# Attention's values for the middle column blocks by DMA, and its first two projection units a stage earlier

## What is computed

```python
h = _rms(x, pre_g) * (1 + scale) + shift                     # for latent and context tokens
q, k, v, g = split(h @ w_in)                                 # 16 heads of 64
s_win = einsum(q, k[row_sel]) * scale + bias                 # window: 8 rows x 16 columns, masked by column
s_ctx = einsum(q, k_ctx) * scale
p = softmax(concat(s_win, s_ctx))
o = einsum(p_win, v[row_sel]) + einsum(p_ctx, v_ctx)
out = (o * silu(g)) @ w_out
```

## Time and profile before

| | us |
|---|---|
| median of 3 runs | 2271.32 (2268.11 to 2275.94) |
| the profiled execution | 2274.24 |
| its span, first to last instruction | 2272.4 |

### The profile page before, as it was taken

How to read it: one execution, slowest core, us unless ns; L and a number is a source line. 1 busy time by engine, 2 the same in 40 slices (tenths; PEclk the granted TensorE clock), 3 DMA queues, 4 the chain that set the end, 5 groups by cost and what they waited for, 6 DMA issues and landing times. The chain is left out here.

```text
span 2272.4 us, 35679 instructions
## 1 busy us (share of the span) xinstructions
PE 2086.1 (92%) x12490; PEld 1717.3 (76%) x12490; DVE 1396.0 (61%) x3285; ACT 1133.4 (50%) x2790; POOL 468.8 (21%) x452
## 2 busy tenths in 40 slices
PE   4699999999999999999976999699999999999797
PEld 2488888787878878787755888577877877877676
DVE  4475968879596887969584433414554554555652
ACT  4244747566573856657363332324544444444431
POOL 1012323233232323323220111310110110110300
PEclk9799999999999999999987999899999999999799
DMA  9512322222221212122127434221211211211433
GB/s 372 202 58 77 98 72 93 74 75 66 83 92 47 102 66 82 60 84 96 38 79 242 126 101 128 65 62 47 71 45 54 74 49 47 75 47 38 151 80 86
DMA packets 118685, 204.70 MB, mean 90 GB/s; under 512 B 29021, under 2 KB 79197, under 8 KB 116461
## 3 DMA queue, kind: packets, MB, share of 16 engines
q1 hardware_dynamic: 106988, 160.47, 22.4%
q10 hardware_dynamic: 11520, 41.95, 5.4%
HBM read 175.69 MB, written 28.65 MB: 90 GB/s over the span
## 5 line engine op out<-in xcount | busy, mean ns | idle before, releaser
L419 PE MATMUL sg_pP<-h_h_hi,h_whi 128*128 128x512 f32 (+1 forms) x1152 | 428.8, 372 | 0.0
L421 PE MATMUL sg_pP<-h_h_hi,h_wlo 128*128 128x512 f32 (+1 forms) x1152 | 410.1, 356 | 0.0
L420 PE MATMUL sg_pP<-h_h_lo,h_whi 128*128 128x512 f32 (+1 forms) x1152 | 409.0, 355 | 0.0
L419 PE MATMUL at_pP<-h_h_hi,at_whi 128*128 128x512 f32 (+1 forms) x640 | 254.4, 397 | 8.4 <-POOL at_wlo L2180 8.4
L421 PEld LDWEIGHTS sg_pP<-h_h_hi,h_wlo 128*128 128x128 f32 x1152 | 218.7, 190 | 31.5
L420 PEld LDWEIGHTS sg_pP<-h_h_lo,h_whi 128*128 128x128 f32 x1152 | 219.4, 190 | 29.6
L419 PEld LDWEIGHTS sg_pP<-h_h_hi,h_whi 128*128 128x128 f32 x1152 | 219.2, 190 | 29.2 <-issue 0.2
L421 PE MATMUL at_pP<-h_h_hi,at_wlo 128*128 128x512 f32 (+1 forms) x640 | 239.0, 374 | 0.0
L420 PE MATMUL at_pP<-h_h_lo,at_whi 128*128 128x512 f32 (+1 forms) x640 | 237.5, 371 | 0.0
L864 ACT ACTIVATE sg_S<-sg_rowb,sg_tab 128x128 f32<-128x128 f32 x640 | 195.9, 390 | 60.9 <-DVE sg_E L1126 56.1
L2180 POOL TENSOR_TENSOR at_wlo<-h_wr,at_whi 128x1024 fp32r<-128x1024 f32 x32 | 76.3, 2383 | 554.0 <-ACT at_whi L2050 554.0
(11 more groups left out here) (319 smaller groups left out, 4553.0 us busy)
## 6 DMA issues: line engine op xcount, KB each, us to landing
sg_rowb<-crows ACTq DMA_DIRECT2D x80, 512.0 KB, 3.7
h_wr<-in_w_ssd SPq DMA_DIRECT2D x48, 512.0 KB, 3.4
fs_w<-in_ada_w SPq DMA_DIRECT2D x16, 1024.0 KB, 8.8
h_wr<-in_w_na SPq DMA_DIRECT2D x32, 512.0 KB, 3.4
at_bias<-bt SPq DMA_DIRECT2D x256, 64.0 KB, 2.3
md_yr<-y SPq DMA_DIRECT2D x40, 256.0 KB, 3.3
fs_w<-in_ada_w SPq DMA_DIRECT2D x16, 512.0 KB, 8.3
y<-sg_Z SPq DMA_DIRECT2D x16, 512.0 KB, 3.0
```

The costliest lines, as they stand in the source:

```text
L419: pe.matmul(out, w_hi[:, k, :], h_hi[:, k, t0:t0 + n], start=(k == 0), stop=False)
L420: pe.matmul(out, w_hi[:, k, :], h_lo[:, k, t0:t0 + n], start=False, stop=False)
L421: x = pe.matmul(out, w_lo[:, k, :], h_hi[:, k, t0:t0 + n], start=False, stop=(k == KT - 1))
```

## The change

Four things, with what they move:

1. `vv` holds only the two outer column blocks (columns 0 to 31 and 32 to 63) and the context. They are transposed in three groups of four, four and two, in tiles qt = 5 to 7 (for pair 0 behind its units). ACT makes two copies per v unit instead of four. The two middle blocks are put together in `vt` by 16 DMAs per pair from the outer ones, issued on SP behind the next pair's first weight load; PE waits for all 16 ahead of a pair's first products with the values.
2. The first attention weights are loaded, split and multiplied inside `middle`. `whi` and `wlo` are kept from the stages before, and `middle`'s ring of y halves lies partly in them. The last input tile goes to `yr` instead, so that the weights can be loaded one tile earlier. ACT splits them ahead of the parts, POOL subtracts ahead of its parts.
3. `EARLY = 2`: the units 0 and 1 of pair 0 (v, tokens 0 to 255 and 256 to 767) run on PE ahead of the last tile's transposes, in the banks that `middle` and `attention` now share. They need the parts 0 and 1, then 2 to 5. ACT does six high halves at the place of five, DVE the low halves of 0, 1, 2 and 5 at the place of 0 to 2, then 6 and 8; POOL those of 3, 4 and 7.
4. Junk output of the last squares goes to the PSUM banks `pt` (so they wait for both halves of the modulation of tile 8), that of the last norm to `G`.

```diff
@@ middle @@
-        pa = [[m.ps(f"pa{i}{h}") for h in range(2)] for i in range(3)]
+        pa = [[m.ps(f"pa0{h}") for h in range(2)], pP, [m.ps(f"pa2{h}") for h in range(2)]]
...
-                if t + 1 < N:
+                if t + 2 < N:
                     sp.dma_start(x, x_in(t + 1)).then_inc(xl, 16)
-                else:
+                elif t + 2 == N:
+                    sp.wait_ge(yls, len(parts))
+                    sp.dma_start(turned(N - 1), x_in(N - 1)).then_inc(xl, 16)
                     sp.dma_start(xw[:, :, :], a["w_na"][0]).then_inc(first, 16)
...
+            pe.wait_ge(fwl, 1)
+            pe.wait_ge(sc, 2 * (N - 2))
+            for q in range(EARLY):
+                t0, n = BLOCKS[q]
+                pe.wait_ge(dlo, (2, 4)[q])
+                if q:
+                    pe.wait_ge(plo, 2)
+                project(pe, pP[q][:, 0:n], whi0[:, 0], wlo0[:, 0], h_hi, h_lo, t0, n)
             turns(N - 1)
...
+                if t == N - 1:
+                    act.wait_ge(h3, t)
+                    act.wait_ge(h3d, t)
                 for h in range(2):
-                    act.activation(turned(t)[:, h * NH:(h + 1) * NH], pa[t % 3][h][:, :], ACT.Square,
+                    junk = turned(t)[:, h * NH:(h + 1) * NH] if t < N - 1 else pt[h][:, :]
+                    act.activation(junk, pa[t % 3][h][:, :], ACT.Square,
                                    accum_out=st[:, h:h + 1]).then_inc(sqs, 1)
...
                 if t == N - 2:
-                    for i in range(5):
+
+                    act.wait_ge(first, 16)
+                    act.wait_ge(yf, part_at[t, 3] + 1)
+                    act.activation(whi0[:, 0, :, :], xw[:, :, :], ACT.Copy).then_inc(fws, 1)
+                    for i in range(6):
                         part_hi(i)
...
             squares(N - 1)
-            part_hi(5)
             part_hi(6)
+            part_hi(7)
             norm_square(N - 1)
-            part_hi(7)
             part_hi(8)
...
                 if t == N - 1:
+                    pool.wait_ge(fws, 1)
+                    pool.tensor_tensor(wlo0[:, 0, :, :], xw[:, :, :], whi0[:, 0, :, :].bitcast(F32),
+                                       ALU.subtract).then_inc(fwl, 1)
                     part_lo(3)
                     part_lo(4)
...
                 if t == N - 2:
-                    for i in range(3):
+                    for i in (0, 1, 2, 5):
                         part_lo(i)
@@ attention @@
+    RG = GR // 4
+    SIDES = [0, CB - 1]
+    turned_at = [(0, 0, RG), (RG, SIDES[1] * RG, RG), (2 * RG, WIN, JC)]
+    VG = len(turned_at)
     VS = QT - VG
+    pieces = []
+    for cw in range(1, CB - 1):
+        for side in range(2):
+            lo, hi = max(K0C[cw], side * KC), min(K0C[cw] + KC, (side + 1) * KC)
+            pieces += [(cw, side, r * KC + lo - K0C[cw], r * KC + lo - side * KC, hi - lo) for r in range(4)]
...
+            def windows(p):
+                sp.wait_ge(vte, p * VG + 2)
+                for cw, side, dst, src, n in pieces:
+                    sp.dma_start(vt[dst:dst + n, p % 2, cw * RG:(cw + 1) * RG, :],
+                                 vt[src:src + n, p % 2, SIDES[side] * RG:(SIDES[side] + 1) * RG, :]).then_inc(vwin, 16)
...
                     if w:
-                        sp.wait_ge(wls, w)
+                        if w > 1:
+                            sp.wait_ge(wls, w - 1)
                         sp.dma_start(wr[:, :, :], a["w_na"][w]).then_inc(wld, 16)
                     w += 1
+                    if i == 0 and p:
+                        windows(p - 1)
...
+                if qt == 0:
+                    pe.wait_ge(vwin, 16 * len(pieces) * (p + 1))
...
-            for q in range(UPP):
+            for q in range(EARLY, UPP):
                 unit(q)
...
-                        for cw in range(CB):
-                            j = cw * (GR // 4) + (b - 1) * (QR // 4)
+                        for side in range(2):
+                            j = side * RG + (b - 1) * (QR // 4)
                             x = act.activation(vv[:, j:j + QR // 4, :].rearrange("p j (r c) -> p (j r) c", c=KC),
-                                               rows[:, :, K0C[cw]:K0C[cw] + KC], ACT.Copy)
+                                               rows[:, :, side * KC:(side + 1) * KC], ACT.Copy)
```

More of the change, by code:

```diff
@@ L1289, in _, with middle @@
                 norm_late(G - 1, c)
-def middle(nc, a, h_hi, h_lo, xw, y_dram, w_dram, scale, x_in, x_out, mod_rows, mod_cols, st_o, first, runs):
+def middle(nc, a, h_hi, h_lo, pre, pP, y_dram, w_dram, scale, x_in, x_out, mod_rows, mod_cols, st_o, runs):
+    xw, whi0, wlo0 = pre
     NH = D // 2
@@ L1313, in middle @@
         yr = m.sb("yr", [P, 2, HY, P])
-        yhi = m.sb("yhi", [P, RY, HY, P], F32R)
-        ylo = m.sb("ylo", [P, RY, HY, P], F32R)
+        own = [m.sb("yxhi", [P, 2, HY, P], F32R), m.sb("yxlo", [P, 2, HY, P], F32R)]
+        ring = [[wb[:, 1, 0:HY, :], wb[:, 1, HY:KT, :], ob[:, 0, :, :], ob[:, 1, :, :], wb[:, 0, 0:HY, :], wb[:, 0, HY:KT, :]]
+                for wb, ob in zip((whi0, wlo0), own)]
+        yhi, ylo = ring
         o = m.sb("o", [P, D])
@@ L1700, in row_start, with attention @@
     return min(max(r - WR // 2, 0), GR - WR)
-def attention(nc, a, h_hi, h_lo, wr, first, bt_dram, y_dram, mod_rows, x_tile, out_tile, st_o):
+def attention(nc, a, h_hi, h_lo, pre, pP, bt_dram, y_dram, mod_rows, x_tile, out_tile, st_o):
     PR = NAH // 2
@@ L1781, in attention @@
             "mh", "ows", "owls", "gl", "gm", "yhs", "yls", "opd", "sqs", "vr", "rs", "sc", "ad"))
-        pP = [m.ps(f"pP{i}") for i in range(2)]
         pA = [m.ps(f"pA{e}") for e in range(2)]
@@ L2177, in _ @@
         def _(pool):
-            for w in range(PR * len(KINDS)):
-                pool.wait_ge(whs, w + 1)
+            for w in range(1, PR * len(KINDS)):
+                pool.wait_ge(whs, w)
                 pool.tensor_tensor(wlo[:, w % 2, :, :], wr[:, :, :], whi[:, w % 2, :, :].bitcast(F32),
@@ L2362, in program @@
         wr = m.sb("wr", [P, KT, P])
+        whi = m.sb("whi", [P, 2, KT, P], F32R)
+        wlo = m.sb("wlo", [P, 2, KT, P], F32R)
+        pre = (wr, whi, wlo)
         with ExitStack() as inner:
             mi = Mem(nc, inner, "h0")
-            whi = mi.sb("whi", [P, 2, KT, P], F32R)
-            wlo = mi.sb("wlo", [P, 2, KT, P], F32R)
             u = mi.sb("u", [P, UW])
-            pre = (wr, whi, wlo, u)
-            first_stage(nc, a, x0, h_hi, h_lo, pre, pad, mod_rows, mod_cols, kept)
-            ssd_groups(nc, a, h_hi, h_lo, pre, tabs, crows, pad, run, y0)
-        middle(nc, a, h_hi, h_lo, wr, y0, a["w_ssd_out"], a["norm_g"], x0, lambda t: rows(x1, t), mod_rows, mod_cols,
-               stored[0], first, (run, bt))
-        attention(nc, a, h_hi, h_lo, wr, first, bt, y1, mod_rows, lambda b, t: (b, patch(x1[CTX:TOK, :], t)),
+            first_stage(nc, a, x0, h_hi, h_lo, (wr, whi, wlo, u), pad, mod_rows, mod_cols, kept)
+            ssd_groups(nc, a, h_hi, h_lo, (wr, whi, wlo, u), tabs, crows, pad, run, y0)
+        pP = [m.ps(f"pP{i}") for i in range(2)]
+        middle(nc, a, h_hi, h_lo, pre, pP, y0, a["w_ssd_out"], a["norm_g"], x0, lambda t: rows(x1, t), mod_rows, mod_cols,
+               stored[0], (run, bt))
+        attention(nc, a, h_hi, h_lo, pre, pP, bt, y1, mod_rows, lambda b, t: (b, patch(x1[CTX:TOK, :], t)),
                   lambda b, t: (patch(out, t), b), stored[1])
```

62 lines of the change are left out of this document (30 added, 32 removed).

## The result

| | before | after |
|---|---|---|
| median | 2270.53 us (4 runs) | 2255.22 us (2252.41 to 2256.36, 4 runs) |
| the profiled execution | 2274.24 us | 2255.57 us |
| its span | 2272.4 us | 2253.8 us |

The ratio is 0.9925, with an interval from 0.9908 to 0.9941: 17 us saved (13 to 21), where 27.3 were forecast. The profiled execution before lay 2.9 us above the median that the forecast started from (2271.32), the one after 0.35 above its own; so of the 11.2 us between the forecast 2244.0 and the measured 2255.22 the account can explain 8.7 (27.3 - 18.6), and the other 2.5 are differences between executions. One of the 15 executions of the kernel before that stand beside experiments 5 to 8 (2406.97 us, granted clock 0.83) was slow, and the ratios leave it out.

What follows compares the result with a forecast made beforehand. PE was taken to bound attention's tiles (574 of 589 us), idle time the handover; 11.7 + 2.7 + 1.7 + 8.3 + 2.9 = 27.3 us off the median 2271.32 gave 2244.0 us, range 2237 to 2258.

Steps and rivals of the forecast that it cites:

- The step that failed: SP queue behind the 16 added copies per pair: next weight load not due for about 15 us, cost 0.
- The price of an issue: SP's time to issue each added copy, taken from the 64 KB bias loads: 0.53 us, 8.4 us for sixteen.
- The handover: Between middle and attention: two early units fill PE's gap, unit 6 then waits for third weights; 11.7 us won, bounds 8.5 to 13.
- The new wait of PE for POOL ahead of unit 6: Sign that the forecast is right, in the handover: PE newly waits for POOL there, under 3 us.
- DVE's fourth low half: Handover: the added subtraction meets POOL's and delays the last squares by 0.45 us, or 2.7 if POOL's second goes first.
- rival 3: Handover gives only the weights' wait, as DVE's fourth low half comes last (+2.25 us on the squares): 2248 us; chance 0.1.
- The first pair's values and the clock behind them: First pair: two fewer transpose groups save 2.7 us, and the clock not falling behind them saves 1.7 us.
- The later pairs: Tiles 3 and 4 lose 0.59 us each in seven pairs (8.3 us); fewer ACT copies end PE's 0.41 us stall (2.9 us).
- Rival 4: Attention's tiles: the 0.59 us are not PE's own, so only 16.1 us are saved: 2255 us; chance 0.03.
- Rival 1: Tiles 3 and 4: PE's freed time becomes waits on ACT or DVE, 18.6 us saved: 2252.7 us; chance 0.22.
- Rival 2: Each pair's first value products: PE waits for small copies landing one after another; 2329 us at 3 us each; chance 0.05.

Runs made afterwards that it cites:

- experiment 5: The changed kernel again, unaltered, on the chip of experiment 6, experiment 7 and experiment 8: ratio 0.9928 to the kernel before, 2260.22 us.
- experiment 6: experiment 2 with all six early low halves subtracted on DVE and the last squares' junk in the free weight buffer: ratio 0.9855, 2242.41 us.
- experiment 7: The changed kernel with each copy cut in two, 32 of 1 KB per partition instead of 16 of 2 KB: ratio 1.0024, 2278.89 us.
- experiment 8: experiment 6 with the first pair's k weights loaded before the barrier and the g weights ahead of the first bias loads: ratio 0.9869, 2246.41 us.
- experiment 1: The changed kernel with pair 0's 16 copies behind the load of pair 1's k weights on SP: ratio 0.9878, 2248.35 us.
- experiment 2: experiment 1 with pair 7's second bias half also moved behind the first output weight loads: ratio 0.9877, 2249.65 us.
- experiment 4: The changed kernel with the values as before (18 transposes in five groups, four copies per unit, no DMAs), new handover kept: ratio 0.9954, 2267.38 us.

## Why the prediction was right and where it failed

The forecast of 2244.0 us lay 11.2 under the measured 2255.22; sign and range (2237 to 2258) held. The range did not hold for its reasons, though: its upper end was set for a change that does not work in the tiles, and what filled it was a cost that had been put at nothing.

- **The step that failed: "Behind them on SP stands the next weight load, not due before POOL has split the previous ones, about 15 us later. Cost: 0"** For pair 0 that load was due at once: its buffer was free at 1507.3, before the first copy was issued at 1511.2. It waited 16 us, and ACT waited for it with the exponentials behind. Cost 7.0 us net in tile 1, and 1.3 in pair 7 (1.58 in its tile 0, 0.9 to 1.0 in three other executions), where the bias loads and output weights stand behind the copies. Experiments 1, 2, 4 and 7 show it: move the load ahead and the stall is gone, double the number of copies and it more than doubles. The forecast looked at who waits for the copies, found nobody, and took the queue behind them from the steady state. The trace of before could have told: there this load went out as soon as POOL had split the weights ahead of it, and ACT asked for it 14 us later:

```profile
1506.31 11.21 SPq L1856 DMA_DIRECT2D h_wr<-in_w_na  x2
...
1514.78 2.39 POOL L2180 TENSOR_TENSOR at_wlo<-h_wr,at_whi 128x1024 fp32r<-128x1024 f32 x1 [8.49 <-ACT at_whi L2050]
...
1531.27 1.05 ACT L2050 ACTIVATE at_whi<-h_wr 128x1024 fp32r<-128x1024 f32 x1
```

  (The second of the two ends at 1517.5, and POOL at 1517.17.) Sixteen copies behind the second group's evacuation (1521.0) at the forecast's own 8.4 us, and 3.4 to land, make 1532.8: 1.5 late already, and 5.5 at the 12.4 us that they took. And in the changed kernel ACT asks for the load sooner, at 1516.3, 3.8 us behind tile 0's start instead of 5.4.
- **The price of an issue** was taken as 0.53 us from the bias loads; it is 0.77 (and 0.75 at half the size). With 0.53 the stall would have been some 4 us shorter (16 x 0.24), not gone.
- **The handover: 11.7 forecast, 9.8 measured** (10.6 counted from the last two products; the other 0.7 lies ahead of them). Units 0 and 1 fit into the gap and end ahead of the norm; PE waits 1.99 us for it, and the transposes take 1.09 us at full clock, as forecast:

```profile
1458.13 1.09 PE L1468 MATMUL md_pt<-md_ident,md_yr 128*128 128x128 f32 x8 [1.99 <-DVE md_yr L1649]
...
1464.53 0.79 PE L419 MATMUL h_pP<-h_h_hi,h_whi 128*128 128x512 f32 x1 [5.30 <-ACT at_vv L2114]
```

  The third weights were ready at 1485.4 (forecast 1484.85), but PE came to unit 6 only at 1487.0. The clock was low from 1460.2 to 1470.4, and unit 2 took 8.4 us (1464.53 to 1472.91) instead of 5.44. The forecast let only the third weights set unit 6, but they were there 1.6 us before units 2 to 5 had ended. Two things held these units up, and end together: the low clock in unit 2, and the k weights, which unit 3 needs and which the forecast left out. These took 5.2 us from issue (1464.07) to ACT's split (1469.32), and POOL ended at 1472.85, 0.06 us ahead of unit 2. So the clock alone, "little" in the forecast, was indeed little here, and so were the k weights alone; the two together cost up to 1.6 us. The new wait of PE for POOL ahead of unit 6, which the forecast named as a sign, did not come.
- **DVE's fourth low half** cost 0.7 us on the squares in this profile (they waited 1.94 us for the modulation, and 1.23 for PE where nothing else holds them, as in experiment 6), near the 0.45 forecast, and in other executions 2.4 more, the forecast's rival 3. The rule weighed there (the Trainium skill, "SBUF — State Buffer", Who interferes with whom) agrees with the traces in that the other engine is held while one works (DVE's fourth 2.54 us and not 1.23); which of the two goes first differed between executions.
- **The first pair's values and the clock behind them**: 4.4 forecast, 5.3 measured. Tile 0 alone gave 1.74, against the 1.7 of the clock, and the clock is indeed what changed: 1.00 from 1511.6 to 1520.0, and 0.50 again in experiment 4, with the five groups back. The guess in the middle of its bounds was a choice, not a reading.
- **The later pairs**: 11.2 forecast (8.3 and 2.9), 11.9 measured. Tiles 3 and 4 are shorter by 0.61 and 0.59, and the second tile by 0.55 (10.45 to 9.90) in pairs 1 to 6: PE's 0.41 us wait is gone there and a little with it. There are 80 value transposes, as forecast.
- **Rival 4** (the 0.59 us are not PE's own, 2255) met the measured number, by chance: periods 3 and 4 gave all of it, and the 0.41 us wait went too. **Rival 1** (PE's time given back, 2252.7) was near for the same wrong reason. **Rival 3** (DVE's fourth half last) is what happens in two of seven profiles, and costs 3.7 us at unit 6 there. **Rival 2** (the value products wait for the copies) did not occur, not even with 32 copies; its place was right (small copies are dear), its victim was not.

## What to carry to other kernels

A DMA had two prices here: landing, which overlaps with others (16 bias loads were issued in 8.4 us though each took 2.3 to land), and issue, which holds everything behind it in the same queue. Sixteen small copies cost 12 us of SP's queue, and halving their bytes did not make one cheaper (0.75 us against 0.77); before adding such copies, list what stands behind them there, when each of these could go out today, and who waits for it, for the first and last iteration by themselves. Two things that end together hide each other: taking one away gains nothing until the other goes too. And when an edit removes idle time ahead of a barrier, look at what clock the work behind it will get.

## What was not expected of the hardware

- A copy within SBUF of 24 or 8 partitions x 2 KB holds SP for 0.77 us and one of half that size for 0.75, against 0.46 to 0.53 for a 64 KB bias load from DRAM (16 in 7.36 us after, in 8.42 before). The shape of the copies does not explain it by bytes; what does is open.
- When DVE and POOL both have 128x1024 subtractions ready, which one goes first is not the same in all executions: five profiles one way, two the other, 2.4 us on the squares and 3.7 on unit 6 between the two profiles of the changed kernel.
- Six such subtractions took DVE 7.57 us alone; beside POOL's two, DVE's four took 7.3 to 9.7. All six were done 9.5 or 9.7 us behind the first one's start when shared (1439.88 to 1449.41, 1442.64 to 1452.35), so POOL's help there was worth nothing.
- The 512 KB load issued right behind the barrier took 5.2 us to ACT's start on it, where the median to landing on the profile's page is 3.4; why was not tested.
